# Attention with past keys and values: who issues the loads of past values, and when the keys and values of this step are stored

## What is computed

```python
past_sel  = cache_slc_kv[page_table[b]]        # 2 pages of 128 rows: keys and values of the selection branch
past_win  = state_win_kv[b]                    # 256 rows: keys and values of the window branch
o_c = softmax(q @ kc[b] + bias) @ vc[b]        # compressed blocks, from on-chip sums
o_s = softmax(q @ [past_sel.k, new.k] + bias) @ [past_sel.v, new.v]
o_w = softmax(q @ [past_win.k, new.k] + bias) @ [past_win.v, new.v]
o   = g0 * o_c + g1 * o_s + g2 * o_w           # gates of each head
h   = h + rmsnorm(o @ w_o)                     # output projection
```

## Time and profile before

| | |
|---|---|
| median of 3 runs | 2634.51 us (2634.45 to 2635.32) |
| the profiled execution | 2629.14 us, of which the span is 2627.5 us |
| TensorE busy | 2540.3 us (97% of the span) |
| VectorE, ScalarE, GpSimd busy | 1212.5, 913.5, 291.6 us |
| granted clock of TensorE, mean | 0.988 of full speed |
| transfers | 403.36 MB, mean 154 GB/s |

### The profile page before, as it was taken

The page is one execution under the profiler, slowest core; times in us unless marked ns, Lnnn a source line. Parts: engine busy times, 40 slices in busy tenths (PEclk is TensorE's granted clock), DMA queues, the critical chain, the costliest instruction groups (busy, mean ns, idle before and its releaser), DMA issues.

```text
span 2627.5 us, 44090 instructions
## 1 busy us (share of the span) xinstructions
PE 2540.3 (97%) x17340; PEld 2484.0 (95%) x17340; DVE 1212.5 (46%) x1372; ACT 913.5 (35%) x1130; POOL 291.6 (11%) x324
## 2 busy tenths in 40 slices
PE   8799999999999999999999789999999999999997
PEld 6799999999999999999997579899999999999997
DVE  6564444444444444643434544644444444444444
ACT  3354333323322333532324443533233233323332
POOL 2430000000000001300002221300000000000012
PEclk9899999999999999999999899999999999999999
DMA  6524444444444444445445534334444444444443
GB/s 250 177 96 146 155 162 145 153 152 158 157 146 163 153 144 149 139 157 175 158 177 163 164 128 144 128 135 144 159 159 152 148 162 153 135 166 162 144 151 128
DMA packets 88810, 403.36 MB, mean 154 GB/s; under 512 B 13245, under 2 KB 23885, under 8 KB 58931
## 3 DMA queue, kind: packets, MB, share of 16 engines
q1 hardware_dynamic: 82594, 390.06, 43.5%
q0 software_dynamic: 6160, 12.60, 1.5%
HBM read 394.88 MB, written 19.02 MB: 158 GB/s over the span
## 4 chain that ended last, share of the span: by engine, by line
PE 85%; DVE 5%; ACT 3%; SPq 3%; DMA 2%; issue 2%; POOL 0%; DVEq 0%; ACTq 0%
PE ps L1285 27%; PE ps L1286 27%; PE ps L1287 27%; ACT w_hi L477 1%; DMA pastK<-win_k_dram 1%; SPq L361 1%; DVE w_lo L740 1%; PE ps L1376 1%; PE ps L1463 1%; DVE winB L847 1%; DVE winA L847 0%; ACT y L585 0%; ACT x_hi L503 0%; PE ps L1549 0%; PE ps L1608 0%
## 5 line engine op out<-in xcount | busy, mean ns | idle before, releaser
L1285 PE MATMUL ps<-x_hi,w_hi 128*128 128x320 f32 x3536 | 1095.1, 310 | 7.6 <-DVE sg L911 4.1
L1287 PE MATMUL ps<-x_hi,w_lo 128*128 128x320 f32 x3536 | 1093.1, 309 | 0.0
L1286 PE MATMUL ps<-x_lo,w_hi 128*128 128x320 f32 x3536 | 1093.1, 309 | 0.0
L740 DVE TENSOR_TENSOR w_lo<-w_raw,w_hi 128x2048 fp32r<-128x2048 f32 (+1 forms) x364 | 749.0, 2058 | 654.3 <-ACT w_hi L477 654.3
L477 ACT CAST w_hi<-w_raw 128x2048 fp32r<-128x2048 f32 (+1 forms) x364 | 623.2, 1712 | 534.0 <-PE ps L1287 475.3
L1285 PEld LDWEIGHTS ps<-x_hi,w_hi 128*128 128x128 f32 x3536 | 664.2, 188 | 9.9 <-DVE sg L911 4.6
L1286 PEld LDWEIGHTS ps<-x_lo,w_hi 128*128 128x128 f32 x3536 | 664.2, 188 | 0.4 <-issue 0.2
L1287 PEld LDWEIGHTS ps<-x_hi,w_lo 128*128 128x128 f32 x3536 | 664.1, 188 | 0.0
L1287 PE MATMUL ps<-hid_hi,w_lo 128*128 128x320 f32 x1408 | 435.1, 309 | 0.0
L1285 PE MATMUL ps<-hid_hi,w_hi 128*128 128x320 f32 x1408 | 435.1, 309 | 0.0
L1286 PE MATMUL ps<-hid_lo,w_hi 128*128 128x320 f32 x1408 | 435.1, 309 | 0.0
(11 more groups left out here) (234 smaller groups left out, 1529.6 us busy)
## 6 DMA issues: line engine op xcount, KB each, us to landing
w_raw<-w_in_dram SPq DMA_DIRECT2D x176, 1024.0 KB, 4.9
w_raw<-w_out_dram SPq DMA_DIRECT2D x128, 704.0 KB, 4.0
w_raw<-w_kv_dram SPq DMA_DIRECT2D x24, 1024.0 KB, 6.2
w_raw<-w_q_dram SPq DMA_DIRECT2D x17, 1024.0 KB, 4.9
w_raw<-w_o_dram SPq DMA_DIRECT2D x15, 1024.0 KB, 4.9
win_out_dram<-win_kv_dram POOLq DMA_DIRECT2D x8, 992.0 KB, 5.2
rowsK<-cmp_data_dram SPq DMA_DIRECT2D x16, 256.0 KB, 9.3
w_raw<-w_pool_dram SPq DMA_DIRECT2D x4, 1024.0 KB, 7.1
```

The costliest lines, as they stand in the source:

```text
L740: V.tensor_tensor(w_lo[:, slot, 0:width], src, w_hi[:, slot, 0:width].bitcast(F32), ALU.subtract).then_inc(lo_made, 1)
L1285: M(out, wh, xh[:, k, :], start=(k == 0), stop=False)
L1286: M(out, wh, xl[:, k, :], start=False, stop=False)
L1287: last = M(out, wl, xh[:, k, :], start=False, stop=(k == kt - 1))
```

## The change

SP keeps the loads of keys and runs one sample ahead with them. The values of samples 1 to 7 are issued by ScalarE, behind its copy of the output rows of the sample before. The eight stores of keys and values move out of the attention: each now follows one of the first eight of the 14 panels of `w_o` that SP loads during the output projection, a loop that is written out.

```diff
-        for b in range(DB):
-            load_keys(b)
-            load_values(b)
-            part = slice(b * N_KVT // DB, (b + 1) * N_KVT // DB)
-            sp.dma_start(kv_out[:, part, :], kvT[:, part, :]).then_inc(rows_out, 16)
-            if b == 0:
-                sp.wait_ge(crow_sum, 2)
-                panel(P_WO, 0, w_o[0], PW)
+        load_keys(0)
+        load_values(0)
+        sp.wait_ge(crow_sum, 2)
+        panel(P_WO, 0, w_o[0], PW)
+        load_keys(1)
+        for b in range(1, DB):
+            if b < DB - 1:
+                load_keys(b + 1)
             if b == DB // 2:
                 sp.wait_ge(s_made, place(PW // NT) + 1)
                 sp.dma_start(w_rawY[:, :], w_o[1]).then_inc(raw_in[(P_WO + 1) % 2], 16)
 
-        with sp.Fori(1, KT // 2) as i:
-            for j in range(2):
-                panel(P_WO + j, i, w_o[i * 2 + j], PW)
+        for i in range(2, KT):
+            panel(P_WO + i, 0, w_o[i], PW)
+            if i < DB + 2:
+                part = slice((i - 2) * N_KVT // DB, (i - 1) * N_KVT // DB)
+                sp.dma_start(kv_out[:, part, :], kvT[:, part, :]).then_inc(rows_out, 16)
...
+        def page(p):
+            return act.value_load(pgs[0:1, p:p + 1], min_val=0, max_val=slc_kv.shape[0] - 1)
+
         def out_rows(p):
 
             act.wait_ge(o_made, p + 1)
             nc.scalar.copy(oN[:, :], ps[:, 6 + p % 2, 0:P]).then_inc(oN_made, 1)
+            b = unit(p) - NH + 1
+            if b < DB:
+                act.wait_ge(o_made, place(NH + b - 1) + 1)
+                for n in range(NPG):
+                    act.dma_start(pastV[:, 0, n, :], slc_kv[page(b * NPG + n), :, 1, :]).then_inc(pastV_in, 16)
+                act.dma_start(pastV[:, 1, :, :], win_kv[b, :, 1, :].rearrange("(t p) n -> p t n", p=P)).then_inc(pastV_in, 16)
```

## The result

The first comparison gave 2595.95 us for the change (4 executions, 2593.98 to 2596.38) and 2634.48 us for before (4, 2633.53 to 2635.32): a ratio of 0.9852 with a 95% interval of 0.9835 to 0.9869, 38.5 us less. Measured again later, beside other executions of before, the change came to 2597.3 against 2630.5 us, a ratio of 0.9873 (0.9857 to 0.9890), 33.2 us less.

The account below looks back on a forecast made before the run. TensorE's main multiplications bound the kernel, with waits for past keys in the attention as the change's target. 33.3 - 0.3 - 0.5 = 32.5 us off the 2634.5 us median gave 2602 us, range 2597 to 2612.

Parts of the forecast that it names:

- What bounds it: Whole kernel: TensorE's main multiplications, four fifths of the chain; in the attention, 22.3 us in six waits for past keys.
- keys alone on SP: Attention: all six waits for keys go, periods of 13.59 us, gaining 32.0 us, plus 1.3 us in the last sample's step.
- the sum: All terms together: 33.3 - 0.3 - 0.5 = 32.5 us of gain.
- Values issued by ScalarE: Attention: ScalarE's next exponentials start 0.25 us later, covered except behind the last sample; cost 0.3 us.
- the late values: Attention: keys and values in flight together, once with `w_rawY`; values barely in time, cost 0 to 1 us, taken as 0.5.
- The cover that the sum relied on: Attention: VectorE asks for the exponentials' sums only after the next unit's scores, so 2.0 us of lateness are covered.
- The stores: Output projection: eight stores behind panels of `w_o`, with 8.3 us to spare per panel; cost 0.
- the cover: Output projection: a panel of `w_o` lands 8.3 us before ScalarE begins to round it.
- its two deductions: Costs taken off the 33.3 us: 0.3 us for ScalarE issuing values, 0.5 us for keys and values in flight together.
- Rival 1: Attention: ScalarE's issuing takes 5.3 us instead of 2.66, costing 6.5 us: 2608.5; chance 0.16 together with Rival 2.
- Rival 2: Attention: only issuing time is saved, shared DMA engines eat the rest; gain 26 us, 2608; chance 0.16 together with Rival 1.
- Rival 3: Output projection: stores hold the panels, TensorE stands still in eight tiles and its clock falls; about 2640; chance 0.03.
- rival 4: Attention: TensorE waits for past values instead of keys; 2632; chance 0.03 within 0.2%, 0.02 between 2612 and 2629.

Follow-up runs that it names:

- the four and eight reads: The change with four, or eight, more page reads by ScalarE ahead of each sample's values: 2598.4 us with four, 2611.3 us with eight.

## Why the prediction was right or wrong

*What bounds it, and keys alone on SP.* Right. The undelayed period read in one place of the old trace (13.59 us) came out as 13.67 six times; the step went from 6.17 to 4.87 us. Keys were issued 4.7 us into the step, a little ahead of the 5 to 6 said, and landed 4.0 to 5.3 us later; and the rows put a sample's scores at S + 2.01, not at S + 2.06. Neither changes the sum. The gains were 31.5 us of 32.0, and 1.3 of 1.3.

*Values issued by ScalarE, 0.3 us, and the late values, 0.5 us.* Both came to nothing. The exponentials are not late at all. ScalarE's queue reads the first page number at 1419.4, while the exponentials still run (the copy to `oN` begins at 1420.13):

```profile
L694 ACTq TENSOR_LOAD <-pgs x14: 275/278/468, 1419.4 to 1502.5; - x14
```

So only 1.9 us of the block fall behind `oN`, less than the 2.4 that are free there. The last sample's step, where the 0.3 us should have shown, took 21.08 us, and 21.09 with all transfers back on SP. The cover that the sum relied on was real, as the four and eight reads show. The values were in time with `w_rawY` in flight, at 228 GB/s over that period and up to 419 in a slice; the 266 GB/s that the prediction took from the end of a burst was no limit.

*The stores.* Right, cost 0. Only with all eight at once was the cover used up, and even that showed in no time.

*The step that failed* is the one from the profiled execution to the median: "the median of the runs lies 5.4 us above, and 2634.5 - 32.5 = 2602". It carries before's distance of 5.4 us over to the change, whose profiled execution lay only 2.0 us from its median. That is 3.4 of the 6.0 us by which the gain was missed. Another 2.3 us came from ahead of the attention, where the start of sample 1's scores varied from 1414.2 to 1416.9 us over twelve profiles of all kernels, and 0.3 us is the sum itself (32.8 us between the profiles instead of 32.5). The distance was no constant of the measurement: it was one execution against four others that all lay high. The other 44 of before have a median of 2631.7 us. The range's low end, 2597, took 5 us off the 2602 for scatter. That was too little, because the 5.4 us in the 2602 were scatter too; 2596.6 us, the figure against the profiled execution, was the better forecast of the median.

Part of this scatter belongs to the six standstills: 2.2 of the 3.6 us between the two profiles of before lie in the periods that have them. But it does not all go with them. The 28 executions of the six kernels here without a wait for keys (the change and its variants, the one with eight reads left out) spread over 6.6 us (standard deviation 1.7), the 48 of before over 8.9 (2.5). The stretches that vary by 1.5 to 3 us on their own, shown under the change's repeat, are in all of them.

In the repeat the gain is 33.2 us against 33.3 for the sum without its two deductions. So the mechanism and its size were right, and the translation to the median was wrong. How near the repeat comes to the sum is partly luck: the interval of its ratio is some 4 us wide to either side.

*Rivals.* Rival 1 (ScalarE slow) needed 3.9 us more of reading to appear. Rival 2 didn't occur: no wait for keys is left. The rule of the Trainium skill ("DMA: Bandwidth & Descriptors", "Issuing engines are not separate DMA queues") is right about the engines: spreading transfers over several of them saves no more than the time of issuing. The runs agree: with all transfers on SP the time is the same (2595.35 us), and ScalarE's part of the change buys nothing. The forecast drawn from it was wrong, because the gain lies in what stands ahead in an ordered queue, and no spreading was needed to change that. Rival 3 (the projection pays) and rival 4 (values late) didn't occur.

What stays open: why the first four executions of before were all high. A chip's own level is possible (up to 2.8 us between three chips; the first comparison's chip isn't on record). Chance alone is unlikely, since 10 of the 44 later executions reach 2633.5 us, and four of four would be about one case in 400. Open as well is what decides whether the clock falls behind a standstill of 1 to 3 us.

## What to carry to other kernels

In a queue that works in order, put the request whose buffer is free first ahead of the one whose buffer is free later; look for a wait behind which something stands that needn't wait. The distance between one profiled execution and a median of few is scatter: don't carry it over to the new kernel, but put it into the range on both sides. Compare two profiles stretch by stretch, and set aside what differs in the stretches that the change doesn't touch. A standstill can cost more than its length: behind all six of before came a stretch at the low clock. A period that happens to run undelayed once in the old trace came within 0.1 us of the new one.

## What the hardware did that I had not expected

ScalarE's queue reads registers and starts transfers while earlier exponentials are still being computed: the reads took 278 ns at the median and began 0.7 us ahead of the copy to `oN` that stands before them. Up to 2 us more of them delayed nothing but the last sample's step, by 0.9 us. 2.74 us of useless multiplications in each of six standstills made the kernel 13 us faster, because five of the six steps behind them ran wholly at 2.4 GHz instead of partly at 1.2. And the same standstill of 1.72 us, ahead of the same instructions, was followed by the full clock in eight profiles and by a stretch at the low clock in four, 1.66 us longer.
